# Seven Strassen products for the gate tiles too, in three of the seven steps of each up map

## What is computed

```python
def conv_ffn(h, w_up, w_dw, b_dw, w_down):
    up = jnp.einsum("bsd,df->bsf", h, w_up)
    act, gate = up[..., :D_FF], up[..., D_FF:]
    act = causal_dwconv(act, w_dw, b_dw)
    return jnp.einsum("bsf,fd->bsd", jax.nn.silu(act) * gate, w_down)
```

## Time and profile before

| | us |
|---|---|
| median of three runs | 929.39 |
| lowest, highest | 929.23, 931.12 |
| the profiled execution | 928.98 |
| its span in the profile | 927.2 |

### The profile page before, as it was taken

How to read it: one execution, slowest core, us unless ns; L and a number is a source line. 1 busy time by engine, 2 the same in 40 slices (tenths; PEclk the granted TensorE clock), 3 DMA queues, 4 the chain that set the end, 5 groups by cost and what they waited for, 6 DMA issues and landing times.

```text
span 927.2 us, 13912 instructions
## 1 busy us (share of the span) xinstructions
PE 916.2 (99%) x5532; PEld 791.6 (85%) x5532; DVE 613.3 (66%) x819; ACT 430.2 (46%) x645; POOL 139.2 (15%) x110
## 2 busy tenths in 40 slices
PE   8999999999999999999999999999999999999997
PEld 7888898888889999988888898888999999888887
DVE  6999986579986666756343468899676666633333
ACT  7653566456444445563222455563545445422330
POOL 0574834000000000056000020000000002800000
PEclk9999999999999999999999999999999999999999
DMA  7323030322223332212323341222222332222212
GB/s 262 116 91 115 9 110 21 117 91 92 69 87 117 93 136 91 92 63 94 125 68 118 112 136 52 95 105 68 92 92 99 125 123 80 94 89 98 93 63 91
DMA packets 22616, 90.03 MB, mean 97 GB/s; under 512 B 2976, under 2 KB 6304, under 8 KB 19104
## 3 DMA queue, kind: packets, MB, share of 16 engines
q1 hardware_dynamic: 21984, 88.72, 28.2%
q10 hardware_dynamic: 576, 0.52, 0.2%
HBM read 86.09 MB, written 2.10 MB: 95 GB/s over the span
## 4 chain that ended last, share of the span: by engine, by line
PE 97%; POOL 1%; DMA 1%; issue 0%; SPq 0%; ACT 0%; DVE 0%; DVEq 0%
PE bank L1530 18%; PE bank L1531 18%; PE bank L1532 18%; PE bank L1843 6%; PE bank L1844 6%; PE bank L1845 5%; PE bank L1823 5%; PE bank L1822 5%; PE bank L1821 5%; PE bank L1572 2%; PE bank L1590 1%; PE bank L1958 1%; DMA w_raw<-w_pw 1%; PE bank L1596 0%; PE bank L1926 0%; PE bank L1607 0%
## 5 line engine op out<-in xcount | busy, mean ns | idle before, releaser
L1043 DVE TENSOR_TENSOR w_lo<-w_raw,w_hi 128x1408 fp32r<-128x1408 f32 (+2 forms) x53 | 99.2, 1872 | 70.2 <-ACT w_hi L604 69.3
L1531 PE MATMUL bank<-u_lo,w_hi 128*128 128x512 f32 (+1 forms) x374 | 140.8, 377 | 0.0
L604 ACT ACTIVATE w_hi<-w_raw 128x1408 fp32r<-128x1408 f32 (+2 forms) x59 | 93.8, 1590 | 98.5 <-PE bank L1532 97.5
L480 POOL TENSOR_TENSOR u_lo<-u_sum,late_hi 128x512 fp32r<-128x512 f32 x32 | 52.1, 1670 | 488.3 <-ACT late_hi L909 488.3
L1530 PE MATMUL bank<-late_hi,w_hi 128*128 128x512 f32 (+1 forms) x272 | 102.6, 377 | 0.0
L1532 PE MATMUL bank<-late_hi,w_lo 128*128 128x512 f32 (+1 forms) x272 | 102.4, 377 | 0.0
L1530 PE MATMUL bank<-f_hi,w_hi 128*128 128x512 f32 x240 | 94.0, 392 | 0.0
L1532 PE MATMUL bank<-f_hi,w_lo 128*128 128x512 f32 x240 | 93.4, 389 | 0.0
L1531 PE MATMUL bank<-f_lo,w_hi 128*128 128x512 f32 x240 | 93.4, 389 | 0.0
L1843 PE MATMUL bank<-as_is,w_hi 128*128 128x512 f32 x224 | 88.3, 394 | 0.0
L1844 PE MATMUL bank<-as_is,w_hi 128*128 128x512 f32 x224 | 88.2, 394 | 0.0
(11 more groups left out here) (262 smaller groups left out, 2178.3 us busy)
## 6 DMA issues: line engine op xcount, KB each, us to landing
w_raw<-w_up SPq DMA_DIRECT2D x56, 512.0 KB, 4.4
w_raw<-w_down SPq DMA_DIRECT2D x32, 704.0 KB, 4.0
w_raw<-w_up SPq DMA_DIRECT2D x16, 1024.0 KB, 4.9
w_raw<-w_pw SPq DMA_DIRECT2D x11, 1024.0 KB, 5.1
x_res<-x SPq DMA_DIRECT2D x3, 512.0 KB, 7.2
out<-out_sb SPq DMA_DIRECT2D x12, 128.0 KB, 2.1
w_raw<-w_pw SPq DMA_DIRECT2D x4, 256.0 KB, 7.0
gathered<-stage SPq DMA_DIRECT2D x32, 32.0 KB, 2.3
```

What stands on the lines that cost most here:

```text
L604: nc.scalar.activation(w_hi[s][:, 0:columns], w_raw[s][:, 0:columns], ACT.Copy).then_inc(w_rounded[s], 1)
L1043: V.tensor_tensor(w_lo[s][:, 0:columns], w_raw[s][:, 0:columns], as_f32(w_hi[s][:, 0:columns]), SUB).then_inc(w_split[s], 1)
L1531: M.matmul(dst, a, lo, start=False, stop=False)
```

## The change

In the steps i = 5, 7 and 9 (`FULL`) of each layer the two gate tiles are computed as the act tiles are, by seven products of 256 columns (`gate_product`), in place of the eight chunks. The other four Strassen steps (4, 6, 8, 10) stay, with `HALF_STEPS` for the counts. The gate products have their own four slots for weight operands, laid into the room of `w_hi[1]` and `w_lo[1]` (`gate_hi`, `gate_lo`, `gate_sum`), so a slot is free for a full step only when the chunks of the step ahead have read their half, and the halves of the step behind wait for the gate's last products. The new functions `round_gate_op`, `copy_gate` (ScalarE), `add_gate_weights` and `split_gate_op` (VectorE) are the gate's counterparts of the act tiles' functions. Partial results go to `rms`, to a half of `sumsq` and to `u_sum`. Some semaphores were merged into counting ones (`weights_added`, `bank_copied`), with the same meaning.

```diff
+FULL = (5, 7, 9)
+HALF_STEPS = FAST - len(FULL)
+GATE_SLOTS = (0, 2, 1, 3, 0, 2, 1)
+FULL_TURNS = (("act", 1), ("gate", 1), ("act", 5), ("gate", 5), ("act", 6), ("gate", 6), ("act", 3), ("gate", 3), ("act", 7), ("gate", 7),
+              ("act", 2), ("act", 4), ("gate", 2), ("gate", 4))
+ADDED = {5: 1, 6: 2, 3: 3, 7: 4}
+FIRST, FIFTH, SECOND, LOW = 1, 2, 3, 4
...
+        gate_hi = [place(f"gate_hi{n}", [P, KH, P], f32r, RING_AT + 4 * UNIT * 2 + 4096 * n) for n in range(RING)]
+        gate_lo = [place(f"gate_lo{n}", [P, KH, P], f32r, RING_AT + 4 * UNIT * 2 + 4096 * n + 2048) for n in range(RING)]
+        gate_sum = [place(f"gate_sum{n}", [P, KH, P], f32, RING_AT + 4 * UNIT * 2 + 4096 * n + 2048) for n in range(RING)]
...
+        def gate_slot_free(queue, layer, i, n):
+            if n < RING:
+                queue.wait_ge(gate_done, 2 * half_of(layer, i - 1) + (1 if n < 2 else 2))
+            else:
+                queue.wait_ge(gate_product_done, PRODUCTS * full_of(layer, i) + n - RING + 1)
...
                         elif u == 0:
-                            sp.wait_ge(sum3, before)
+                            sp.wait_ge(weights_added, 4 * before)
                             sp.wait_ge(op_split, job(layer, i - 1, PLACE[1]) + 1)
+                        elif i - 1 in FULL:
+                            sp.wait_ge(gate_weights_added, 4 * full_of(layer, i))
                         else:
-                            sp.wait_ge(gate_split, 2 * before - 1)
+                            sp.wait_ge(gate_split, 2 * half_of(layer, i) - 1)
...
                         if i > PLAIN and u == 0:
                             sp.wait_ge(op_split, job(layer, i - 1, PLACE[4]) + 1)
+                        elif i > PLAIN and i - 1 in FULL:
+                            sp.wait_ge(gate_op_split, PRODUCTS * full_of(layer, i))
                         elif i > PLAIN:
-                            sp.wait_ge(gate_split, 2 * before)
...
+            def round_gate_op(layer, i, product):
+                n, step, before = PLACE[product], step_of(layer, i), full_of(layer, i)
+                slot = GATE_SLOTS[n]
+                gate_slot_free(act, layer, i, n)
+                if product in (1, 2, 4):
+                    act.wait_ge((near_loaded if product == 1 else far_loaded)[1], 16 * (step + 1))
+                    source = raw_block(0 if product == 1 else 1, 1 if product == 4 else 0, 1)
+                else:
+                    act.wait_ge(gate_weights_added, 4 * before + ADDED[product])
+                    source = gate_sum[slot][:, :, :]
+                nc.scalar.activation(gate_hi[slot][:, :, :], source, ACT.Copy).then_inc(gate_op_rounded, 1)
+            def copy_gate(layer, i, which):
+                before = full_of(layer, i)
+                product = {FIRST: 1, FIFTH: 5, SECOND: 6, LOW: 4}[which]
+                edge, low = gate_bank(i, 0), gate_bank(i, 1)
...
+                    if i + 1 in FULL:
+                        round_gate_op(layer, i + 1, 1)
+                    else:
+                        round_gate(layer, i + 1, 0)
                     round_op(layer, i + 1, PLACE[6])
+                    if i + 1 in FULL:
+                        round_gate_op(layer, i + 1, 5)
                 act.wait_ge(edge_added, after)
...
+            def full_step(layer, i):
+                after = step_of(layer, i) + 1
+                silu(layer, i - 1, 1)
+                copy_first(layer, i)
+                round_gate_op(layer, i, 6)
+                copy_gate(layer, i, FIRST)
+                round_gate_op(layer, i, 3)
+                copy_fifth(layer, i)
+                round_op(layer, i, PLACE[7])
+                round_op(layer, i, PLACE[2])
+                copy_gate(layer, i, FIFTH)
+                round_gate_op(layer, i, 7)
+                copy_second(layer, i)
+                round_op(layer, i, PLACE[4])
+                round_gate_op(layer, i, 2)
+                copy_gate(layer, i, SECOND)
+                round_gate_op(layer, i, 4)
+                round_op(layer, i + 1, PLACE[1])
+                round_op(layer, i + 1, PLACE[5])
+                round_op(layer, i + 1, PLACE[6])
+                act.wait_ge(edge_added, after)
+                conv_middle(layer, i, 0)
+                round_gate(layer, i + 1, 0)
+                copy_low(layer, i)
+                act.wait_ge(corner_added, after)
+                act.wait_ge(bank_copied, 4 * after)
+                conv_middle(layer, i, 1)
+                silu(layer, i, 0)
+                round_op(layer, i + 1, PLACE[3])
...
+                before = full_of(layer, i)
+                if t == 0:
+                    dve.wait_ge(gate_product_done, PRODUCTS * before + PLACE[2] + 1)
+                    dve.wait_ge(gate_copied, 4 * before + SECOND)
+                    V.tensor_tensor(u_sum[:, 2 * i, :], gate_bank(i, 0)[:, :], gate_first_two, ADD).then_inc(gate_added, 1)
+                else:
+                    dve.wait_ge(gate_copied, 4 * before + LOW)
                 dve.wait_ge(silu_done[t], UP_STEPS * layer + i + 1)
-                dve.wait_ge(gate_done, 2 * (step_of(layer, i) + 1))
-                V.tensor_tensor(u_sum[:, 2 * i + t, :], gate_bank(i, t)[:, :], y[:, t, :], MUL).then_inc(gate_used[t], 1)
+                dve.wait_ge(gate_added, 2 * before + 2)
+                V.tensor_tensor(u_sum[:, 2 * i + t, :], u_sum[:, 2 * i + t, :], y[:, t, :], MUL).then_inc(gate_used[t], 1)
...
+            def full_step(layer, i):
+                after, before = step_of(layer, i) + 1, full_of(layer, i)
+                use_gate(layer, i - 1, 0)
+                add_gate_weights(layer, i, 6)
+                split_gate_op(layer, i, 5)
+                use_gate(layer, i - 1, 1)
+                add_gate_weights(layer, i, 3)
+                split_gate_op(layer, i, 6)
+                add_weights(layer, i, 7)
+                split_gate_op(layer, i, 3)
+                split_op(layer, i, 7)
+                add_gate_weights(layer, i, 7)
+                split_op(layer, i, 2)
+                split_gate_op(layer, i, 7)
+                split_op(layer, i, 4)
+                split_gate_op(layer, i, 2)
+                split_gate_op(layer, i, 4)
+                dve.wait_ge(product_done, job(layer, i, PLACE[7]) + 1)
+                dve.wait_ge(bank_copied, 4 * (after - 1) + FIFTH)
+                V.tensor_tensor(act_in[:, 1, 2 + HT:2 + T], bank[BANK_LOW][:, 0:HT], fifth, ADD).then_inc(corner_added, 1)
+                add_weights(layer, i + 1, 5)
+                split_op(layer, i + 1, 1)
+                dve.wait_ge(gate_product_done, PRODUCTS * before + PLACE[7] + 1)
+                dve.wait_ge(gate_copied, 4 * before + FIFTH)
+                V.tensor_tensor(u_sum[:, 2 * i + 1, HT:T], gate_bank(i, 1)[:, 0:HT], gate_fifth, ADD).then_inc(gate_added, 1)
+                add_weights(layer, i + 1, 6)
+                dve.wait_ge(product_done, job(layer, i, PLACE[2]) + 1)
+                dve.wait_ge(bank_copied, 4 * (after - 1) + SECOND)
+                V.tensor_tensor(act_in[:, 0, 2:2 + T], bank[BANK_EDGE][:, :], first_two, ADD).then_inc(edge_added, 1)
+                split_op(layer, i + 1, 5)
+                conv_rest(layer, i, 0)
+                add_weights(layer, i + 1, 3)
+                split_op(layer, i + 1, 6)
+                split_gate(layer, i + 1, 0)
+                conv_rest(layer, i, 1)
+                split_op(layer, i + 1, 3)
...
+                if i + 1 in FULL:
+                    split_gate_op(layer, i + 1, 1)
+                    add_gate_weights(layer, i + 1, 5)
+                elif not last:
                     split_gate(layer, i + 1, 0)
                 conv_rest(layer, i, 0)
...
+            def gate_product(layer, i, which):
+                n, before = PLACE[which], full_of(layer, i)
+                edge, low = gate_bank(i, 0), gate_bank(i, 1)
+                if which == 1 and i == FULL[0]:
+                    wait_drained((2, 3), DRAINED_UP[layer] + PLAIN)
+                pe.wait_ge(gate_op_split, PRODUCTS * before + n + 1)
+                if which == 1 and before:
+                    pe.wait_ge(gate_copied, 4 * before)
+                if which == 5 and before:
+                    pe.wait_ge(gate_added, 2 * before)
+                if which in (6, 7, 3):
+                    pe.wait_ge(gate_copied, 4 * before + {6: FIRST, 7: SECOND, 3: FIFTH}[which])
+                if which == 4:
+                    pe.wait_ge(gate_added, 2 * before + 1)
+                half = slice(HT, T) if which in (5, 3) else slice(0, HT)
+                dst = (low if which in (1, 6, 7, 4) else edge)[:, half]
...
+                    if i in FULL:
+                        for tiles, which in FULL_TURNS:
+                            if tiles == "act":
+                                product(layer, i, which)
+                            else:
+                                gate_product(layer, i, which)
+                        continue
```

## The result

| | before | after |
|---|---|---|
| median, us | 929.31 (4 runs) | 948.59 (4 runs) |
| lowest, highest | 929.01, 931.12 | 946.73, 950.77 |
| profiled execution | 928.98 | 948.89 |
| its span | 927.2 | 947.1 |

The changed kernel is slower by a factor of 1.0202 (95% interval 1.0182 to 1.0222). The sign was forecast. The size was not: 939.3 us, with 948.0 as the upper end, and it came out 9.3 us above the forecast and 0.6 above that end. Factors "of before" further down are against runs of before that were taken together with the experiment (their medians are 929.5 to 930.0).

What follows compares the result with a forecast made beforehand. TensorE, busy 916.2 of 927.2 us, was taken as the bound. Saving 0.99 us per full step but adding waits of 0.86 and 1.78 gave +1.65, six times +9.9: 939.3 us on the median of 929.39, range 934 to 948.

Steps and rivals of the forecast that it cites:

- What TensorE saves: In a full step seven products replace eight gate chunks on TensorE: 0.99 us less, 5.9 us over six steps.
- First wait, gate product 5: At the gate's product 5 in a full step TensorE waits 0.75 us for VectorE's split, 0.86 with the restart.
- T: The start of a full step, from which the prediction counts its times in us.
- The walk to the far load: VectorE's queue from the gate's split 5 to operand 4's split, done at T + 11.95, when SyncE may load.
- The landing: Second half of the next act weights lands 3.6 to 3.7 us after issue, at T + 15.65; VectorE waits 1.35.
- the three signs of being wrong: VectorE's edge addition earlier in the step than walked, far load issued before T + 11, or either wait missing.
- Product 1, "about 0.25 early": In the step behind a full one, product 1's operand comes about 0.25 us before TensorE needs it.
- Second wait, product 6: In the step behind a full one TensorE waits 1.67 us for ScalarE's copy of product 1, 1.78 with restart.
- The sum: Per full step and the one behind: -0.99 + 0.86 + 1.78 = +1.65 us; six give +9.9, so 939.3 us.
- Loads decide: Rival: shifted loads land late in most full steps, 2.5 us more each, 954 us; chance 0.10 (up to 956).
- One us in each of them is +6: Bound: each microsecond of load lateness in a full step lands on TensorE; one in each gives 945.3 us.
- The clock rival: Rival: 1.2 GHz for half of each fast step behind a wait, 60 us more, 999; chance 0.03 with dearer products.

## Why the prediction was wrong, by its own steps

**What TensorE saves: right.** Gate products start 1.44 us apart (1.435 forecast); a full step without waits is 20.15 us, so 0.93 us are saved and not 0.99. The six full steps could give 5.6 us.

**First wait, gate product 5: right in place, cause and size.** In step 7 it is 0.86. The tap's stall is there: VectorE waited 1.47 us for ScalarE (forecast 1.6) and began its taps at T - 1.97 (forecast T - 1.96):
```profile
337.23 0.75 DVE L1351 SCALAR_TENSOR_TENSOR y<-act_in,par,y 128x512 f32<-128x512 f32 x1 [1.47 <-ACT y L835]
```
Moving the rounding from ahead of the tap removed the wait. In layer 1 it was 1.04 to 1.11 ahead of the restart, which the working did not have: 1.0 us in all. In step 5 ScalarE's rounding begins 1.06 us behind the sum there, where it has 0.78 in layer 0; why is not shown.

**The walk to the far load: right.** Issued at T + 11.93, forecast T + 11.95.

**The landing: this step failed.** "That transfer lands 3.6 to 3.7 us after its issue in its usual case, at T + 15.65" is the wrong term. It landed after 4.4 to 4.9 us in all six full steps, at T + 16.5 to 17.2, and VectorE waited 2.20 us in step 7, in place of 1.35. VectorE in after:
```profile
353.20 0.43 DVE L1553 TENSOR_TENSOR act_in<-bank,sumsq 128x256 f32<-128x256 f32 x1 [0.79 <-PE bank L2018]
355.84 0.69 DVE L1455 TENSOR_TENSOR ring_sum<-w_raw 128x512 f32<-128x512 f32 x1 [2.20 <-DMA w_raw<-w_up]
```
I took the landing from steps in which the loads go out in close pairs. In a full step the near load of the gate tile goes out alone, 2.2 us ahead of the far act load, and I never asked what that does. With that load cut to an eighth the far one lands after 3.4 to 3.8 us, and the Strassen steps cost what I forecast to 0.5 us. So the gate tile's near load is the cause here. How it delays the far one is not shown. That it is still moving is not enough: in before it goes out 2.4 us ahead of the far act load, in a close pair, and lands 2.1 us after that one's issue (2.2 in after), and yet the far load landed after 3.6 us. What the traces show beside this is the rate, the last number of these stretches in GB/s, from the issue of the gate's near load to the landing of the far act load, first in before, then in after:
```profile
297.65:303.64 5.99, 5.99 (x41) 5.47 (x41) 1.99 (x3) 2.27 (x5) 0.00 (x0) 1.00 0.87 314
```
```profile
348.89:355.71 6.82, 6.82 (x59) 6.82 (x58) 3.68 (x6) 3.26 (x7) 0.00 (x0) 1.00 0.71 231
```
None of the three signs of being wrong that the prediction names came true, and none of them was about the landing.

**Product 1, "about 0.25 early": wrong by the late landing.** The slack of 0.25 turned into a wait of 0.48 to 1.04 (distances of starts), the third line of TensorE's waits. That is how the late landing reaches TensorE, and it lengthened the full step from 20.95 to 21.7 and more.

**Second wait, product 6: right.** 1.87 and 0.08 in the restart against 1.67 and 0.11. With the early landing it was 1.4 to 1.8, so it took a smaller part of the lateness than product 1, where TensorE had already waited. ScalarE's copy stands behind silu and rounding, as forecast:
```profile
365.11 0.63 ACT L840 ACTIVATE y<-y 128x512 f32<-128x512 f32 x1 [2.15 <-DVE y L1353]
365.64 1.04 ACT L911 ACTIVATE w_hi<-w_raw 128x1024 fp32r<-128x1024 f32 x1
366.59 0.37 ACT L947 ACTIVATE sq<-bank 128x256 f32<-128x256 f32 x1
```
**The sum.** -0.93 + 0.86 + 1.95 = 1.88 per pair, six times 11.3, then 4.8 for the wait of product 1 and 1.0 for layer 1's longer first wait make 17.1; 17.2 were measured. A further 2.0 us in the profiled execution came from ahead of the Strassen parts, and 0.7 from behind them: profiled executions of these kernels start their Strassen part between 271.0 and 273.2 us, whatever the edit, and I had no term for either. Two slips in the working changed nothing: VectorE's work in a full step starts from 13.9 us where the earlier trace rows has 14.4 (the sum of 19.2 then would be 19.7; after shows 17.9 busy in 22 us), and 945.3 + 2.5 is 947.8, not 947.

**The rivals and the range.** "Loads decide" was the right rival with the wrong price: I charged it 2.5 us for each landing, from the one late pair, and so put it at 954. "One us in each of them is +6", under the bounds, was the right slope, and the run with the cut load measured it as 6.3. The range should have had that as its middle and not as its edge, since in the changed kernel a landing beyond 3.7 us was the rule. The clock rival did not come true in the changed kernel. Two stretches of after, one full step and the one behind it, us, busy us of each engine, granted clock (behind GpSimd's), DMA:
```profile
339.00:361.00 22.00, 20.89 (x171) 20.47 (x170) 17.91 (x29) 11.84 (x24) 0.00 (x0) 1.00 0.29 96
361.00:384.00 23.00, 21.30 (x133) 18.96 (x134) 17.00 (x26) 11.27 (x21) 0.00 (x0) 1.00 0.26 92
```
TensorE stood for 1.1 and 1.7 us in them and the clock stayed at 1.00, the 2.4 GHz level; in the whole of after it falls only in the last 4 us, and so it does in before. The rule of the Trainium skill that the prediction cites ("TensorE: Matmul & The Clock Gate", "A second HAM failure mode: psum-queue depth-cycling") would have had it oscillate; the trace disagrees here, with its waits of up to 1.9 us. But the rival was not far away. The granted clock fell to 0.50 for 3.4 us three times in these experiments, within 1 us of the end of a wait: twice with the copies moved, at waits of 2.0 and 2.3 us (distances of starts), and once with the roundings of late chunks moved forward, at the wait of 2.5 us that ends at 412.17. At the 2.3 us of that last run's layer 1 it did not fall. The mean granted clock of a whole run hides this: it is 0.996 or more in every one.

## What to carry to other kernels

When a change moves a load to another place in its queue, its landing is an unknown, also if its size and number stay: a landing read from another pattern of issues is not the landing in the new one, and the range has to carry the difference. Where a chain of operations has a slack of a few tenths at one operand, price the error of every external term against that slack, since it turns into a wait on all repetitions at once. Look for the clock in short stretches behind the longest waits, not in the mean of the run. And ask of every instruction that fills an idle place on one engine what it releases on the next: ScalarE's rounding of a sum stalled VectorE's taps, and its rounding of late chunks set off GpSimd beside VectorE.

## What the runs showed of the hardware

- The far act load, 512 KB, issued alone 2.2 us behind one of the same size that was issued alone too, landed after 4.4 to 4.9 us, eighteen of eighteen in the changed kernel and in the runs with the tap and with the copies moved, and after 4.2 and 5.6 in the run with one full step. With an eighth of the bytes ahead of it, after 3.4 to 3.8. In before, where it follows by 2.4 us the second load of a close pair, it landed after 3.5 to 4.1 us in ten of twelve steps, and after 4.4 and 6.1 in the others.
- With the gate's near load 0.4 us behind it instead of 2.2 ahead, the same load took 3.5 to 6.1 us. The latest, 5.0 twice, 5.5 and 6.1, were all in step 7 of layer 0, in four kernels; two others had 4.0 and 4.1 there. The cause is not shown.
- VectorE's operations of 128 x 512 with two operands in SBUF take 0.69 us alone (the taps 0.75) and mostly 1.67 to 1.79 while GpSimd runs its splits. Those with one operand in PSUM keep 0.68 to 0.69 in the same stretches.
- At waits of 2.0 and 2.3 us in one run and of 2.5 in another TensorE's granted clock went to 0.50 for 3.4 us, and matmuls of 256 columns started 0.21 us apart instead of 0.12. Waits of up to 1.9 us in the changed kernel did not bring that, nor did one of 2.3 us in the other run's layer 1.
